# Attention bias rows asked for on ScalarE's queue into three raw buffers, and GpSimd's bias sums ahead of its last mixer tables

## The reference, cut to what matters

```python
col_in = (kcol[None, :] >= col_start[:, None]) & (kcol[None, :] < col_start[:, None] + NA_KW)
mask = ...
bias = rpb[:, dr_idx][:, :, dc_idx]
...
s_loc = jnp.einsum('bqhd,bkhd->bhqk', qr, kb) * scale + bias
s_loc = jnp.where(mask, s_loc, NEG_INF)
p = jax.nn.softmax(jnp.concatenate([s_loc, s_ctx], axis=-1), axis=-1)
```

## Time and profile before

| | before |
|---|---|
| median of 3 runs | 1913.64 us |
| lowest, highest | 1910.66, 1914.75 us |
| the profiled execution's own time | 1914.57 us |
| its span | 1912.7 us |
| mean granted TensorE clock | 0.977 of full speed |
| TensorE busy, share of the span | 95% |
| VectorE, ScalarE, GpSimd | 66%, 52%, 16% |
| DMA, mean | 252 GB/s |
| latent steps of the first attention (185.6 to 232.85 us from the start) | 47.2 us |
| its context steps (to 262.25 us) | 29.4 us |

### The profile page before, as it was taken

How to read it: one execution, slowest core, us unless ns; L and a number is a source line. 1 busy time by engine, 2 the same in 40 slices (tenths; PEclk the granted TensorE clock), 3 DMA queues, 4 the chain that set the end, 5 groups by cost and what they waited for, 6 DMA issues and landing times.

```text
span 1912.7 us, 25247 instructions
## 1 busy us (share of the span) xinstructions
PE 1814.9 (95%) x8938; PEld 1413.6 (74%) x8938; DVE 1265.6 (66%) x1329; ACT 1003.7 (52%) x1096; POOL 312.3 (16%) x584
## 2 busy tenths in 40 slices
PE   4999788999999989797999999999999999999998
PEld 2666444888888876465888888888888888888886
DVE  3243734442433234744998989989889898898997
ACT  3222423421312121363677767777777777776774
POOL 6887931011111124101000000000000000000000
PEclk8999899999999999897999999999999999999999
DMA  9788532122323151502799999999989999898994
GB/s 371 307 337 272 195 127 88 43 111 77 121 77 121 45 203 56 165 2 88 289 370 355 352 370 337 368 352 355 371 344 359 349 358 368 346 362 345 364 367 182
DMA packets 72374, 481.55 MB, mean 252 GB/s; under 512 B 8368, under 2 KB 11568, under 8 KB 17456
## 3 DMA queue, kind: packets, MB, share of 16 engines
q1 hardware_dynamic: 68720, 470.82, 64.5%
q0 software_dynamic: 2448, 7.61, 1.5%
q10 hardware_dynamic: 1136, 2.21, 0.4%
HBM read 473.29 MB, written 7.32 MB: 251 GB/s over the span
## 4 chain that ended last, share of the span: by engine, by line
PE 90%; DMA 3%; DVE 3%; POOL 2%; issue 1%; ACT 1%; SPq 0%; DVEq 0%; ACTq 0%; POOLq 0%
PE bank L1042 32%; PE bank L1056 16%; PE bank L775 12%; PE bank L745 4%; PE bank L804 3%; PE bank L792 3%; PE bank L625 3%; PE bank L840 2%; DMA ring<-in_ev_mod 2%; PE bank L563 2%; PE bank L1015 2%; PE bank L1025 1%; PE bank L713 1%; PE bank L605 1%; PE bank L696 1%
## 5 line engine op out<-in xcount | busy, mean ns | idle before, releaser
L1806 DVE TENSOR_TENSOR rest<-ring,WR 128x2048 fp32r<-128x2048 f32 x336 | 758.3, 2288 | 80.6 <-ACT WR L1373 80.1
L1373 ACT ACTIVATE WR<-ring 128x2048 fp32r<-128x2048 f32 x336 | 632.3, 1917 | 48.4 <-DMA ring<-in_experts 47.9
L1042 PE MATMUL bank<-WR,xer 128*128 128x512 f32 x1792 | 582.0, 397 | 0.8 <-DVE s5v L1967 0.8
L1042 PEld LDWEIGHTS bank<-WR,xer 128*128 128x128 f32 x1792 | 337.0, 188 | 70.3 <-issue 0.8
L1042 PE MATMUL bank<-rest,xer 128*128 128x512 f32 x896 | 349.5, 390 | 0.0
L1056 PE MATMUL bank<-WR,heTr 128*128 128x512 f32 x896 | 282.2, 392 | 0.0
L775 PE MATMUL bank<-hTr,WR 128*128 128x512 f32 x672 | 207.2, 390 | 0.0
L1056 PEld LDWEIGHTS bank<-WR,heTr 128*128 128x128 f32 x896 | 168.2, 188 | 34.6
L1042 PEld LDWEIGHTS bank<-rest,xer 128*128 128x128 f32 x896 | 169.1, 189 | 32.9
L1056 PE MATMUL bank<-rest,heTr 128*128 128x512 f32 x448 | 174.4, 389 | 0.0
L1658 DVE TENSOR_TENSOR rest<-ring,WR 128x2048 fp32r<-128x2048 f32 (+2 forms) x38 | 80.3, 2115 | 123.9 <-ACT WR L1298 123.6
(11 more groups left out here) (338 smaller groups left out, 2175.4 us busy)
## 6 DMA issues: line engine op xcount, KB each, us to landing
ring<-in_experts SPq DMA_DIRECT2D x336, 1024.0 KB, 4.8
ring<-in_ev_mod SPq DMA_DIRECT2D x24, 1024.0 KB, 9.0
ring<-in_od_mod SPq DMA_DIRECT2D x24, 1024.0 KB, 8.6
ring<-in_ffn_up SPq DMA_DIRECT2D x22, 1024.0 KB, 6.8
ring<-in_ffn_down SPq DMA_DIRECT2D x12, 768.0 KB, 5.1
ring<-in_ev_in SPq DMA_DIRECT2D x8, 1024.0 KB, 6.7
ring<-in_ev_out SPq DMA_DIRECT2D x4, 1024.0 KB, 8.5
ring<-in_od_out SPq DMA_DIRECT2D x4, 1024.0 KB, 13.5
```

The source lines that it names most:

```text
L1042: mm = pe.matmul(bank[m % 2][:, :], xer[:, i, 4 * kh + k, :], w[j][:, 512 * k:512 * k + 512], start=(kh == 0 and k == 0 and x == 0), stop= ...
L1373: act.activation(part(0, h), ring[:, h % HALVES, :], ACT.Copy).then_inc(split_hi, 1)
L1806: dve.tensor_tensor(part(1, h), ring[:, h % HALVES, :], part(0, h).bitcast(F32), ALU.subtract).then_inc(split_lo, 1)
```

## The change

The raw rows of a head are asked for by ScalarE instead of GpSimd, into three raw buffers instead of two. ScalarE issues loads 0, 1 and 2 after its work on outputs 8, 9 and 12 of the input projection, loads 3 and 4 in the Fourier part right ahead of the copies `TQ` of v = 5 and 6, and loads 5, 6 and 7 at the head of steps 1, 2 and 3 of the attention. A load from the fourth on first waits until the bias that used its buffer is made (`bias_ready`). GpSimd's program loses all 32 issues; its biases 4 to 7 move ahead of tables: 2, 3, table 12, 4, 5, table 13, 6, 7, tables 14 and 15. The rest of the program is the same.

```diff
-        bias_raw = B[:, 8192:9216].rearrange("p (b n) -> p b n", b=2)
+        bias_raw = [B[:, at:at + 512] for at in (8192, 8704, 10368)]
...
+            def load_bias(h):
+
+                if h >= 3:
+                    act.wait_ge(bias_ready, h - 2)
+                for t in range(2):
+                    for q in range(2):
+                        src = bass.AP(a["rpb"].tensor, (h * NA_DR + 7 - 2 * t - q) * RPB_PAD,
+                                      [[1, GRID_W], [RPB_PAD, ROWS], [1, GRID_W]])
+                        act.dma_start(bias_raw[h % 3][64 * q:64 * q + 64, t * SEQ:(t + 1) * SEQ]
+                                      .rearrange("p (r c) -> p r c", r=ROWS), src).then_inc(bias_landed[h % 3], 16)
...
+                if j in (8, 9, 12):
+                    load_bias((8, 9, 12).index(j))
...
                     act.wait_ge(four_b, v + 1)
                     if v >= 2:
                         act.wait_ge(four_o, v - 1)
+                    if v in (5, 6):
+                        load_bias(v - 2)
                     act.activation(TQ[:, v % 2, :], bank[(6, 2)[v % 2]][:, 256:256 + HALF_F], ACT.Copy).then_inc(four_q, 1)
...
                 for r in range(n + 1):
+                    if steps is EVEN_STEPS and 1 <= r < 4:
+                        load_bias(4 + r)
...
             def head_bias(h):
 
-                if h + 1 < NA_HEADS:
-                    if h >= 1:
-                        pool.wait_ge(bias_ready, h)
-                    load_bias(h + 1)
-                pool.wait_ge(bias_landed[h % 2], 64 * (h // 2 + 1))
+                pool.wait_ge(bias_landed[h % 3], 64 * (h // 3 + 1))
...
             for k in range(8, 12):
                 table(k)
-            head_bias(2)
-            head_bias(3)
-            for k in range(12, 16):
+            for h in range(2, NA_HEADS):
+                head_bias(h)
+                if h in (3, 5):
+                    table(12 + h // 4)
+            for k in range(14, 16):
                 table(k)
-                head_bias(k - 8)
```

More of the change, by code:

```diff
@@ L313, in build @@
         four_a, four_t, four_b, four_q, four_o = sem("four_a"), sem("four_t"), sem("four_b"), sem("four_q"), sem("four_o")
-        bias_landed = [sem("bias0_landed"), sem("bias1_landed")]
+        bias_landed = [sem("bias0_landed"), sem("bias1_landed"), sem("bias2_landed")]
         bias_ready, bias_used = sem("bias_ready"), sem("bias_used")
@@ L2103, in _ @@
             pool.wait_ge(s5_raw, 32)
-            def load_bias(h):
-                for t in range(2):
-                    for q in range(2):
-                        row = 2 * t + q
-                        src = bass.AP(a["rpb"].tensor, (h * NA_DR + 7 - row) * RPB_PAD,
-                                      [[1, GRID_W], [RPB_PAD, ROWS], [1, GRID_W]])
-                        pool.dma_start(bias_raw[64 * q:64 * q + 64, h % 2, t * SEQ:(t + 1) * SEQ]
-                                       .rearrange("p (r c) -> p r c", r=ROWS), src).then_inc(bias_landed[h % 2], 16)
-            def head_bias(h):
-                if h + 1 < NA_HEADS:
-                    if h >= 1:
-                        pool.wait_ge(bias_ready, h)
-                    load_bias(h + 1)
-                pool.wait_ge(bias_landed[h % 2], 64 * (h // 2 + 1))
+            def head_bias(h):
+                pool.wait_ge(bias_landed[h % 3], 64 * (h // 3 + 1))
                 if h == 2:
@@ L2126, in head_bias @@
                 b = bias[h % 4].rearrange("p (r c) -> p r c", c=GRID_W)
-                raw = bias_raw[:, h % 2, :].rearrange("p (r c) -> p r c", c=GRID_W)
+                raw = bias_raw[h % 3].rearrange("p (r c) -> p r c", c=GRID_W)
                 pool.tensor_tensor(b, raw[:, :, ::-1], cst[:, C_MASK:C_MASK + GRID_W].unsqueeze(1)
@@ L2156, in _ @@
                 table(k)
-            load_bias(0)
             for h in range(2):
```

## The result

The changed kernel takes 1919.25 us (median of seven runs, 1917.4 to 1924.72), the kernel before 1910.73 us on the same chip (1908.79 to 1914.75). The ratio is 1.0045, 95% interval 1.0032 to 1.0058: slower by 8.5 us, where 1911.0, that is 2.6 us faster, and a range of 1904 to 1918 were forecast. The profiled execution of the changed kernel is the slowest of its seven (1924.72), that of the kernel before is near its slowest (1914.57); the times in the views are of these two, 10.2 us apart.

The account below looks back on a forecast made before the run. TensorE filled 90% of the chain; the change could reach GpSimd's 39.4 us from bias 2. Context steps at 230.1, 2.7 us sooner, less 0.1 in the projection, gave 1911.0 us against the median, range 1904.0 to 1918.0.

Parts of the forecast that it names:

- GpSimd's work, 39.4 to 18.4 us: Attention, bias 2 to bias 7: six biases and two tables remain on GpSimd, 21 us less than before.
- ScalarE's issues, 0.44 us each: Fourier part and attention: 1.8 us a head; loads 3 and 4 delay the Fourier part's end by 3.6 us.
- Packets and landings: Attention's row loads: 256-byte packets alternate with the ring's, 0.40 us a turn, 0.05 free; bias 4 at 206.6, bias 5 at 214.3.
- own pace: Rival for the attention: all rows land in time between ring loads; gain 8.7 us, 1904.9 us; chance 0.35.
- Steps 2 and 3 lose some 0.6 each: Attention: loads 5 to 7 ahead of exponentials, beyond ScalarE's idle time, cost steps 2 and 3 together 1.2 us.
- With the issues gone I count this stall as gone: Attention: VectorE's operation at 188.90, 4.17 us where its likes take 0.5, no longer stalls.
- The stall at 172.04, and 0.7 us back: Fourier part: VectorE's 2.87 us stall after a table's DMA moves away, giving back about 0.7 us.
- 2.8 us later, as it does now: Attention: the step after step 4's second head at 214.3 starts 2.8 us later, step 5 at 217.1.
- The own pace: Attention, Fourier part's end to context steps: eight steps of 4.05 us plus some 2 us for modulation, 34.4 us.
- 0.1 us in the input projection: Input projection: rows of heads 0 and 1 share engines with a ring load; up to 0.5 us, 0.1 taken.
- Later stages unchanged: From the output projection on: any gain or loss in the attention should reach the end whole.
- stuck behind the ring: Slower rival, attention: load 4 lands at 211 to 212, load 7 holds step 3's exponentials; 1917.6 us; chance 0.22.

Follow-up runs that it names:

- e3: The changed kernel with each row transfer read as 64 runs of 1 KB instead of 256 of 256 bytes (wrong rows, same bytes): 1902.3 us.
- e8: The changed kernel with loads 6 and 7 issued behind the exponentials of steps 3 and 4, not ahead of those of steps 2 and 3: 1917.75 us.
- e9: Against the kernel before: all rows issued early by GpSimd, two six-row transfers a head, tables 12 to 15 behind bias 7: 1898.61 us, ratio 0.9930.
- e12: Against the kernel before: two six-row transfers a head on ScalarE, all before the Fourier part, tables 12 to 15 behind bias 7: 1899.76 us, ratio 0.9934.
- e7: The changed kernel with two transfers of six rows a head instead of four of four, 768 packets and half the issues: 1912.69 us.

## Why the prediction was wrong

The miss in three stages, in the two profiled executions: bias 2 comes 1.3 us later than forecast, from it to the context steps it takes 49.5 us where 41.6 were forecast (188.5 to 230.1; measured 189.81 to 239.30, VectorE's first context maximum), 7.9 more, and the context steps lose 1.8. Together 11.0 us, of the 11.1 between 2.6 faster and 8.5 slower. By its own steps:

- **GpSimd's work, 39.4 to 18.4 us**: right. From bias 2 to bias 7 it made six biases and two tables in 18.4 us, and idled 14.24 us.
- **ScalarE's issues, 0.44 us each**: too low, the upper end was right. An issue took 0.60 to 0.64 us (median 0.640), so loads 3 and 4 cost 4.2 us and not 3.6: the copy `T1` ahead of them stands at 182.05 us (182.07 before), and bias 2 at 189.81 (185.61).
- **Packets and landings**: one in turn was right (533 and 533). A turn took 16 x 11 / 533 = 0.33 us and not 0.40; the 0.46 that the forecast gave the ring's packets is time that passed, idle stretches included, for the earlier trace rows has 864 packets at 73.4%, 0.31 us each. A free packet of 256 bytes was cheaper than 0.05 us: 2365 in 5 us on 16 engines are at most 0.034. So loads 3 and 4 passed whole in the gap between the ring's slots (2446 packets by 198 us), as the rival "own pace" had it, and bias 4 was ready at 199.0 and not at 206.6. That bias 5 came ready at 214.5 us where 214.3 was forecast is then partly luck: nothing of load 4 stood ahead of it. Counted in order, its last packet would have gone out at some 211.3 us (3075 of 3264 packets by 211); why its rows are there only at 213.25 is not shown.
- **"Steps 2 and 3 lose some 0.6 each"**: this is the step that failed first. The issues were counted as time on ScalarE that depends on nothing. Load 6's last issues took 10.88 us, with the ring's slots passing one for one beside its rows, and step 2's exponentials, whose maxima were there, came at 209.19 where e3 has them at 198.38, from the same first exponential: 10.8 us. It is not the whole miss: e8, in which nothing is held ahead of steps 2 and 3, still takes 45.8 us from bias 2 to the context steps (192.40 to 238.17), 4.2 over the forecast. The forecast let steps 2 and 3 pass and had only step 4's second head wait for bias 5.
- **"With the issues gone I count this stall as gone"**: wrong, and the second step that failed. The issues were only where the division happened to start: others beside issues of rows took 0.49 to 0.69 us before (196.25, 206.37, 214.76, 187.96). What holds it is the unbroken run behind them, and the change made these runs longer (two biases and a table). 4.05 us of it stood in the path at 221.22: the lag behind e3 grows from 10.5 us (step 4's first exponential, 218.19 against 207.68) to 15.0 (step 5's, 226.57 against 211.54).
- **The stall at 172.04, and 0.7 us back**: right. It went, as table 11 now ends at 167.0, and the 0.7 came back: the first copy `T1` is 0.73 us later than before (172.54 to 171.81), the fifth is level (179.41 to 179.44), as TensorE no longer waits between them.
- **"2.8 us later, as it does now" and 12.9 us from step 5 to the context steps**: from bias 5's being ready the forecast had 15.8 us to the context steps (214.3 to 230.1); it was 24.8 (214.5 to 239.3), from steps 2 and 3 having been held, the two stalls, and the clock at its lower level for some 4 us after each wait. Without the hold (e8) it was still 21.3 (216.9 to 238.17). So this term, taken over from the kernel before, failed by itself: after the wait for bias 5 TensorE had a clock of 0.50 for 4 us, a division took 2.16 us, and 1.94 us are the wait behind load 7's issues, which e8 alone has in that place.
- **The own pace**, 34.4 us: near, in the kernels that allow it (e3 34.2, e9 and e12 36.0 from first exponential to context steps). Its rival's time of 1904.9 stands beside 1902.3 of e3.
- **0.1 us in the input projection**: too low. The rows of heads 0 and 1 share the engines with ring loads there, and the projection's last output is copied at 164.91 us and not 164.18, 0.73 later, over the upper end of 0.5. It is one execution of each.
- **Later stages unchanged**: nearly right, 8.27 us at the output projection and 8.5 at 541.61. The context steps however were not unchanged: 30.8 for 28.9 us, at a clock of 0.88 for 0.94.

The rival on the slower side (stuck behind the ring, 1917.6) had the right engine stand with the exponentials behind it, but at load 7 and in a wait for bias 4, which was met in time; the hold came a load earlier and without any wait. The rule of the Trainium skill behind the rival "own pace" (page SBUF — State Buffer, section "SBUF: two separate sides") is that a DMA on a hardware queue runs at full speed beside VectorE's operations. It says nothing of a second hardware queue, and that is what counted here: beside the ring the rows moved 0.13 MB in 11 us. The page DMA: Bandwidth & Descriptors of the Trainium skill, section "Issuing engines are not separate DMA queues", says that DMAs of all issuing engines run on the same 16 DMA engines and interleave. The trace agrees: 533 packets each, 87.9% and 6.3% of the engines' time.

Open: what sets how many rows ScalarE's queue takes before an issue is held. In the changed kernel it came with load 5's and most of load 6's rows outstanding; e7, with three quarters of them, still saw 4.47 and 3.04 us, and e8, with load 5's alone, none over 3.45 us for three. The number outstanding does not decide it alone: from 182.49 us to the start of the held issue (198.90) 15 DMAs of 272 packets were issued and 2485 had gone out, which leaves 1595; by 210.05 it was 17 DMAs and 3031, which leaves 1593, and that issue took 0.64 us. Open too is why the first exponential moves by 2 to 3 us between kernels that are alike up to it.

## What to carry to other kernels

Count a transfer in packets, and ask which queue's packets it will stand beside: on the hardware queues here each short run was a packet and got one turn to the ring's one, whatever its size. Put such loads where the ring leaves gaps and no one waits, long before they are needed; a DMA issue is not a fixed cost, and a held one holds everything that follows on its engine, so it does not belong ahead of work in the critical path. And to shorten one engine's list does not help another that waits for its ports until the runs are shortened or moved: here moving all four tables behind the last bias gave 0.36% with the rows on GpSimd's queue, the change's half of it nothing.

## What the runs showed of the hardware

- A DMA issue on ScalarE took 10.19 us, where most of its likes take 0.60 to 0.67, with some 1600 packets of its queue outstanding beside a busy ring. The profile calls the wait "issue", with no semaphore.
- The turn between two hardware queues is exact (533 and 533), and blind to size: 3.85 MB against 0.13 MB.
- A VectorE row division waited up to 5.84 us, over two biases and four table operations of GpSimd, and was let in where GpSimd itself waited for the end of an operation; others were let in sooner.
- The hold and the division of 4.05 us each cost twice: TensorE, nearly idle in them, works at the lower clock for some 4 us after (0.50 and 0.57). The same 16 matmuls, in the changed kernel after the hold and later:

```profile
212.03 1.97 PE L713 MATMUL bank<-S,B 128*64 128x128 f32 x16
...
218.43 1.09 PE L713 MATMUL bank<-S,B 128*64 128x128 f32 x16
```
